# Two-block forward pass: the recurrent branch in 32x32 blocks with an explicit inverse, six heads a group, with 14 gate tiles and the memory's tiles between its matmuls

## The chip, the cores and the metric

The kernel runs on one core of a Trainium2 chip. The metric is the device time of one execution in microseconds (us). A core has TensorE (PE in the rows; PEld is its weight load), VectorE (DVE), ScalarE (ACT), GpSimd (POOL) and SyncE (SP), which issues most transfers. The engines run side by side and wait for one another by semaphores.

## What is computed

The reference is a model of two blocks over 512 tokens of width 1024. The change is in the second block, in one of its three branches and in what stands beside it:

```python
h = rms_norm(x, norm_mix_g)
(na_q, na_k, na_v, p_r, p_k, p_v, lat_w, lat_a, lat_g, mem_q,
 gate_na, gate_rw, gate_mem) = split_columns(h @ w_in)        # 1024 -> 5888 columns
y_na = neighborhood_attention(...)                            # 6 heads of 64
y_rw = rwkv7_bidirectional(...)                               # 6 heads of 64, two directions
y_mem = memory_attention(mem_q, rms_norm(mem), w_mem_kv)      # 256 memory tokens, 4 heads
merged = sigmoid(gate_na) * (y_na @ w_na) + sigmoid(gate_rw) * (y_rw @ w_rw) + sigmoid(gate_mem) * (y_mem @ w_mem)
x = x + merged @ w_out
x = x + expert_choice_ffn(rms_norm(x), ...)                   # 16 experts
```

The recurrence, for each head, each direction and each token in order:

```python
sa = einsum('vk,k->v', state, a_t)
state = state * w_t + outer(sa, b_t) + outer(v_t, k_t)        # 64 x 64
y_t = einsum('vk,k->v', state, r_t)
```

Then y of both directions is summed, normed by head, added to a bonus and multiplied by a gate.

## The kernel before

The program is a row of stages, each with a barrier at its end: the first block (projections, a state space branch, a gated recurrence, merge and feed-forward), then `front` (projections of the second block and the preparation of the recurrent branch), `attentions` (the two attention branches), `rwkv7` (the recurrent branch), `merge_and_router` and `expert_ffn`. Every large product is three fp32r matmuls (`three_passes`, L68 to L70): high by low, low by high, high by high.

`front` makes 46 tiles of 128 columns by 512 tokens and then 4 tiles of the memory's keys and values by 256 tokens. A tile is 8 steps of three matmuls. For each tile ACT makes the high half of the weights (L2351), DVE the low half (L2507), and DVE evicts the result (L2549). The preparation of the two directions for the recurrent branch runs beside tiles 6 to 18 and 19 to 31; its last piece is the bonus (L2642, L2644). Gate tiles are the last 24 of the 46.

`rwkv7` cuts the tokens into chunks of 32. Inside a chunk the recurrence is a triangular system. The work goes by units: 2 directions x 4 tiles of 128 tokens x 3 pairs of heads = 24 units. The four chunks of a tile lie as diagonal blocks in 128x128 matrices, masked to zero elsewhere (`masks`, L3054). A unit turns four operands (L2905), makes scores (L2911), turns the masked matrix (L2922), and solves the system in five levels (`level`, L2943 to L2945): each level squares the matrix and its transpose and adds A times z to z. To have the sums by chunk, POOL multiplies tokens by a membership mask (`split`, L2816). `finish` (L2964 to L2979) makes for each chunk the transfer matrix (`ht`), its addition (`nn`), the query part (`qt`) and the local output (`y_loc`). Then the scan: 15 steps x 2 directions, each a matmul of the state by the transfer matrix (L3019), one by the queries (L3027), and two DVE operations (L3119, L3122). At last the tail: mean and variance by head through matmuls with a block matrix of ones (L3034, L3037), a logarithm and an exponential on ACT (L2886, L2890), and three DVE operations for each of three tiles. In the tail DVE also splits the attention outputs for the merge, which came back from DRAM (L3134, L3136).

`attentions` runs 20 units (12 windowed, 8 of the memory). Its outputs are stored to DRAM (L1898).

The order on each engine is written out by hand in these functions; semaphores hold them together. The main loop of `rwkv7` on TensorE reads:

```python
for n in range(len(units)):
    level(n, 0)
    if n >= 1: finish(n - 1, 0)
    level(n, 1)
    if n >= 1: finish(n - 1, 1)
    level(n, 2)
    if n + 1 < len(units): front_a(n + 1)
    level(n, 3)
    if n + 1 < len(units): front_b(n + 1)
    level(n, 4)
```

Of the kernel before, what the change touches and what calls it, by code (L numbers as in the profile page):

```python
# [9 lines left out]
P = 128  # L10
ALU = mybir.AluOpType
# [1807 lines left out]
def attentions(nc, stage, na_dram, mem_q_dram, mem_kv_dram, bias_dram, ident_dram, na_out_dram, mem_out_dram):  # L1819
# [11 lines left out]
    with ExitStack() as ctx:  # L1831
# [38 lines left out]
        stored = sem("stored")  # L1870
# [10 lines left out]
        with nc.Block() as block:  # L1881

            @block.sync
            def _(sp):
# [10 lines left out]
                for o, (kind, c) in enumerate(outs):  # L1895
                    sp.wait_ge(y_ready, QT * (o + 1))
                    to = na_out_dram if kind == "na" else mem_out_dram
                    sp.dma_start(to[c * P:(c + 1) * P, :], y[kind][:, c]).then_inc(stored, 16)  # L1898
                sp.wait_ge(stored, 16 * len(outs))
# [77 lines left out]
            def _(dve):  # L1977
# [44 lines left out]
                for n in range(AHEAD):  # L2022
                    soften(n)
                    if n >= 1:
                        weigh(n - 1)
                for n in range(U):
# [4 lines left out]
                    finish(n)  # L2031

            @block.scalar
            def _(act):
# [26 lines left out]
                turned(0)  # L2061
                for n in range(U):
                    if n + 2 < U:
                        exponentials(n + 2)
                    if n + 1 < U:
                        turned(n + 1)

# [38 lines left out]
FRONT_MEM = 33  # L2106


def front(nc, stage, h_dram, mem_dram, gains_dram, mem_gain_dram, w_dram, par_dram, mu_l_dram, lora_dram, ar, bh, kh, v, bonus,
          ends, lat_g, x_dram, p_dram, kv_dram):  # L2110
# [5 lines left out]
    TM = N_MEM  # L2116
    tiles = FRONT_TILES + MEM_TILES
    with ExitStack() as ctx:
        sb, ps, sem = opener(nc, ctx, stage)
        x_high = sb("x_high", [P, KT, T], F32R)  # L2120
        x_low = sb("x_low", [P, KT, T], F32R)
# [4 lines left out]
        scale = sb("scale", [P, T])  # L2126
# [24 lines left out]
        mem = room[:, 0:KT * TM].rearrange("p (k t) -> p k t", k=KT)  # L2151
        mem_sq = room[:, KT * TM:KT * TM + KT * TM // 2].rearrange("p (k t) -> p k t", t=TM)
        mem_sums = sb("mem_sums", [P, 2, TM])
        mem_scale = sb("mem_scale", [P, TM])
        mem_gain = sb("mem_gain", [P, KT])
        with nc.sbuf_tensor(f"{stage}_raw", [P, 3, RW_X, T + 2], F32) as raw, nc.sbuf_tensor(f"{stage}_raw_l", [P, T + 2], F32) as raw_l:
            pass
# [1876 lines left out]
```

## Time and profile before

| what | us |
|---|---|
| median of 3 runs (lowest, highest) | 2938.48 (2933.32, 2939.51) |
| the profiled execution | 2938.72 |
| its span | 2936.3 |

By the rows' own times the second block begins near 1155 us of the span. `front` works until 1448, `attentions` has its first matmul at 1462.25 and its last eviction at 1518.99, `rwkv7` has its units from 1528 to 1803, its scan to 1828 and its tail to 1845, `merge_and_router` goes to about 1952, and the experts take the rest, 984 us, in which the transfer queues are 97% busy. Over the whole span TensorE is busy 91%, VectorE 43%, ScalarE 27%, GpSimd 4%.

How to read it: a matmul's row gives start and modelled length, but matmuls overlap; the distance from one start to the next is what it costs in a stream. A matmul on plain fp32 stands as two records, one on fp32r as one, and so does a transpose. `128*64 128x64` is a weight of 128 rows by 64 columns and a moving operand of 128 rows by 64 columns. Idle time of an engine that isn't the bound costs nothing.

### The profile page before, as it was taken

To read this page: it belongs to the slowest core of one execution; us is meant where nothing else is said; L and a number is where in the kernel's file an instruction comes from. 1 tells how busy PE (TensorE), PEld (TensorE's weight loads), DVE (VectorE), ACT (ScalarE), POOL (GpSimd) and SP (SyncE) were. 2 spreads that over 40 slices of the span, in tenths; PEclk is the share of its full clock that TensorE was granted. 3 is DMA by queue.
4 is the path that set the end of the run, shared out by engine and by line. 5 is a ranking of instruction groups with operands and counts; after the bars stand their busy time and mean duration, and the time that the engine had idled before them with its cause. 6 is when DMAs were issued, how large, how long until landed. Compare 5 with 4: busy or idle time off the path is not lost. (4 is left out here: it accounts for less than half of the span.)

```text
span 2936.3 us, 43512 instructions
## 1 busy us (share of the span) xinstructions
PE 2661.1 (91%) x18294; PEld 1902.3 (65%) x18294; DVE 1257.6 (43%) x2123; ACT 798.0 (27%) x1304; POOL 112.7 (4%) x90
## 2 busy tenths in 40 slices
PE   8997789799999998999789999879988898989887
PEld 8996677699999986778668887654333333333222
DVE  7764656544566633666353336750111111111112
ACT  3220454432343322543253333421000000000001
POOL 0000022000000000000002221000000000000000
PEclk9998899899999999999989999989999999999999
DMA  5447331455322233334510000548999999999996
GB/s 162 131 126 126 110 122 62 149 159 159 116 87 93 73 131 126 122 129 154 177 48 1 2 1 34 192 193 363 431 430 431 431 430 431 431 430 430 431 430 256
DMA packets 144432, 612.44 MB, mean 209 GB/s; under 512 B 37808, under 2 KB 57392, under 8 KB 119216
## 3 DMA queue, kind: packets, MB, share of 16 engines
q1 hardware_dynamic: 120576, 573.72, 50.9%
q10 hardware_dynamic: 23664, 35.95, 3.5%
q8 instruction: 146, 2.39, 0.3%
q14 instruction: 46, 0.38, 0.0%
HBM read 568.48 MB, written 38.78 MB: 207 GB/s over the span
## 5 line engine op out<-in xcount | busy, mean ns | idle before, releaser
L3552 PE MATMUL moe_bank<-moe_ring,xg 128*64 128x512 f32 x2048 | 493.7, 626 | 91.0 <-DMA moe_ring<-in_w_exp_up 90.2
L3552 PEld LDWEIGHTS moe_bank<-moe_ring,xg 128*64 128x64 f32 x2048 | 155.8, 142 | 371.7 <-issue 363.0
L3781 DVE TENSOR_TENSOR moe_sg<-moe_sg,moe_bank 64x512 f32<-64x512 f32 x64 | 44.2, 690 | 584.6 <-ACT moe_sg L3672 584.6
L3580 PE MATMUL moe_bank<-moe_ring,moe_act_t 128*64 128x512 f32 x1024 | 230.6, 592 | 0.5 <-ACT moe_act_t L3679 0.5
L68 PE MATMUL ffn_prod<-ffn_x_low,ffn_w_high 128*128 128x258 f32 x704 | 199.8, 284 | 5.8 <-PEq L144 5.8
L68 PE MATMUL in_bank<-x_low,in_w_high 128*128 128x264 f32 x640 | 186.9, 292 | 16.5 <-DVE in_w_low L983 9.3
L69 PE MATMUL ffn_prod<-ffn_x_high,ffn_w_low 128*128 128x258 f32 x704 | 199.7, 284 | 0.0
L70 PE MATMUL ffn_prod<-ffn_x_high,ffn_w_high 128*128 128x258 f32 x704 | 198.9, 283 | 0.0
L70 PE MATMUL in_bank<-x_high,in_w_high 128*128 128x264 f32 x640 | 184.0, 287 | 0.0
L69 PE MATMUL in_bank<-x_high,in_w_low 128*128 128x264 f32 x640 | 183.7, 287 | 0.0
L3580 PEld LDWEIGHTS moe_bank<-moe_ring,moe_act_t 128*64 128x64 f32 x1024 | 73.3, 137 | 146.4 <-issue 145.8
L3679 ACT COPY moe_act_t<-moe_bank 128x256 f32<-128x256 f32 x64 | 23.8, 372 | 515.9 <-PE moe_bank L3566 515.9
L68 PE MATMUL front_bank<-front_x_low,front_w_high 128*128 128x512 f32 x368 | 148.0, 402 | 12.3 <-DVE front_w_low L2507 12.2
L3789 DVE TENSOR_TENSOR acc<-acc,moe_bank 128x512 f32<-128x512 f32 x128 | 82.1, 683 | 174.3 <-PE moe_bank L3605 174.3
L69 PE MATMUL front_bank<-front_x_high,front_w_low 128*128 128x512 f32 x368 | 144.3, 392 | 0.0
L70 PE MATMUL front_bank<-front_x_high,front_w_high 128*128 128x512 f32 x368 | 144.1, 391 | 0.0
L68 PEld LDWEIGHTS ffn_prod<-ffn_x_low,ffn_w_high 128*128 128x128 f32 x704 | 133.6, 190 | 6.0 <-issue 6.0
L70 PEld LDWEIGHTS ffn_prod<-ffn_x_high,ffn_w_high 128*128 128x128 f32 x704 | 134.0, 190 | 0.0
L69 PEld LDWEIGHTS ffn_prod<-ffn_x_high,ffn_w_low 128*128 128x128 f32 x704 | 133.9, 190 | 0.0
L68 PEld LDWEIGHTS in_bank<-x_low,in_w_high 128*128 128x128 f32 x640 | 122.5, 191 | 17.6 <-issue 9.9
L69 PEld LDWEIGHTS in_bank<-x_high,in_w_low 128*128 128x128 f32 x640 | 123.1, 192 | 0.9 <-issue 0.8
L70 PEld LDWEIGHTS in_bank<-x_high,in_w_high 128*128 128x128 f32 x640 | 122.8, 192 | 0.0
(549 smaller groups left out, 5498.1 us busy)
## 6 DMA issues: line engine op xcount, KB each, us to landing
moe_ring<-in_w_exp_gate SPq DMA_DIRECT2D x64, 2048.0 KB, 27.6
moe_ring<-in_w_exp_up SPq DMA_DIRECT2D x64, 2048.0 KB, 21.3
moe_ring<-in_w_exp_down SPq DMA_DIRECT2D x64, 2048.0 KB, 25.8
front_w<-in_w_in SPq DMA_DIRECT2D x50, 512.0 KB, 3.6
ffn_w<-in_w_up SPq DMA_DIRECT2D x44, 512.0 KB, 4.5
in_w<-in_w_in SPq DMA_DIRECT2D x40, 512.0 KB, 4.2
ffn_w<-in_w_down SPq DMA_DIRECT2D x16, 704.0 KB, 4.0
p<-front_out ACTq DMA_DIRECT2D x35, 256.0 KB, 2.0
```

What stands on the lines that cost most here:

```text
L68: nc.tensor.matmul(to, w_high, x_low, start=start, stop=False)
L69: nc.tensor.matmul(to, w_low, x_high, start=False, stop=False)
L70: return nc.tensor.matmul(to, w_high, x_high, start=False, stop=stop)
L3552: last = nc.tensor.matmul(bank[64 * g:64 * g + 64, s], xe[:, (e // BATCH) % 2, k, at:at + CAPACITY], ring[:, slot_of(n, g), k * HALF:(k + ...
L3580: last = nc.tensor.matmul(bank[64 * h:64 * h + 64, 3 + e % 2], act_t[:, s, j], ring[:, slot, at:at + HALF], start=(c == 0 and j == 0), sto ...
L3679: nc.scalar.copy(act_t[:, s].rearrange("p j n -> p (j n)"), bank[:, 2, s * FT * CAPACITY:(s + 1) * FT * CAPACITY]).then_inc(act_t_ready, 1)
L3781: nc.vector.tensor_tensor(sg[0:CAPACITY, s], sg[0:CAPACITY, s], bank[64:64 + CAPACITY, s], ALU.mult).then_inc(act_ready, 1)
L3789: nc.vector.tensor_tensor(acc[:, FT * h + q], acc[:, FT * h + q], bank[:, part_bank(e, q) + h], ALU.add).then_inc(part_added, 1)
```

## The change

`front` makes only the first 10 gate tiles: 32 tiles in all, no memory tiles. Its rounded operands `x_high` and `x_low`, the scale and the identity are kept for the next stage.

`rwkv7` now comes before `attentions`. Its work goes by groups: 2 directions x 4 tiles of 128 tokens = 8 groups of all six heads. Tokens lie on partitions, 32 to a chunk, so each of the four chunks has its own 32 partitions, and every matrix of a chunk is a 32x32 block at those partitions; the other blocks don't exist, and no membership mask is needed. The system is solved through an explicit inverse: `ch` holds A transposed (AT), the product (PT) and A for each head; five rounds (`chain_round`, L3066, L3070) square A and multiply PT by (I + A^(2^l)). `solve` (L3079) applies the inverse to both right hand sides, `finish_ends` (L3095 to L3106) and `finish_rows` (L3118, L3123) make what `finish` made. Results go where the operands were: the transfer matrices into `ar`, the additions into `bh` and `kh`, the queries into `v`.

Between these pieces TensorE makes `side` work: 14 gate tiles and the 4 memory tiles, 18 x 8 = 144 steps of three matmuls, of which 9 in each group, 2 in each of 30 scan slots, and 3 x 4 in the tail. ACT and DVE split the weights and evict (`side`, `memory`).

`attentions` comes last before the merge. It splits its outputs and the recurrent branch's on chip into `x_high` and `x_low` (8 copies on ACT, 8 subtractions on DVE), loads and splits the first weights of the merge, and stores nothing.

The core of the diff (`...` marks what is left out):

```diff
+FRONT_GATES = 10
+FRONT_UPTO = FRONT_TILES - 3 * KT + FRONT_GATES
-    tiles = FRONT_TILES + MEM_TILES
+    tiles = FRONT_UPTO
...
+SIDE_GATES = 3 * KT - FRONT_GATES
+SIDE_FIRST = 4
+SIDE_TILES = SIDE_GATES + MEM_TILES
+RW_GROUPS = 2 * (SEQ // P)
+GROUP_STEPS = (2, 2, 2, 1, 2)
+SCAN_STEPS = 2
+TAIL_STEPS = 4
+SIDE_STEPS = GROUP_STEPS * RW_GROUPS + (SCAN_STEPS,) * (2 * (RSTEPS - 1)) + (TAIL_STEPS,) * 3
...
             @block.tensor
+                def side(slot):
+                    for q in range(SIDE_UPTO[slot], SIDE_UPTO[slot + 1]):
+                        n, k = divmod(q, KT)
+                        s = n % 2
+                        if k == 0:
+                            pe.wait_ge(w_ready, n + 1)
...
+                            done = three_passes(nc, bank[:, s], w_high[:, s, k], w_low[:, s, k], x_high[:, k], x_low[:, k],
+                                                k == 0, k == KT - 1)
...
+                def chain_round(g, l):
+                    now = ch[:, g % 2, l % 2]
...
+                    first = AT.start if l < LEVELS - 2 else PT.start
+                    upto = AT.stop if l == 0 else PT.stop
+                    for n in range(heads_all):
+                        at = 2 * RCHUNK * n
+                        for c in range(4):
+                            last = nc.tensor.matmul(bank[rows(c), CHAIN_BANK, at + first:at + upto], now[rows(c), n, A],
+                                                    now[rows(c), n, first:upto], start=True, stop=True)
+                        if l < LEVELS - 1:
+                            for c in range(4):
+                                last = nc.tensor.matmul(bank[rows(c), CHAIN_BANK + 1, n * RCHUNK:(n + 1) * RCHUNK], now[rows(c), n, AT],
+                                                        now[rows(c), n, A], start=True, stop=True)
+                    last.then_inc(round_made, 1)
...
+                for g in range(G):
+                    slot = len(GROUP_STEPS) * g
+                    chain_round(g, 0)
+                    if g >= 1:
+                        finish_ends(g - 1)
+                    side(slot)
+                    chain_round(g, 1)
+                    side(slot + 1)
+                    chain_round(g, 2)
+                    if g >= 1:
+                        finish_rows(g - 1)
+                    side(slot + 2)
+                    chain_round(g, 3)
+                    if g + 1 < G:
+                        turn(g + 1, 0)
+                        turn(g + 1, 1)
+                    side(slot + 3)
+                    chain_round(g, 4)
+                    if g + 1 < G:
+                        turn(g + 1, 2)
+                    side(slot + 4)
+                    if g + 1 < G:
+                        scores(g + 1)
+                    solve(g)
+                    if g + 1 < G:
+                        starts(g + 1)
...
             @block.vector
+                def inverse(g, l):
+                    dve.wait_ge(round_made, LEVELS * g + l + 1)
+                    made = bank[:, CHAIN_BANK, 0:2 * heads_all * RCHUNK].rearrange("p (n f) -> p n f", f=2 * RCHUNK)
+                    if l < LEVELS - 2:
+                        nc.vector.tensor_copy(ch[:, g % 2, (l + 1) % 2, :, AT], made[..., AT]).then_inc(inverse_ready, 1)
+                    if l == 0:
+                        return
...
+                    nc.vector.tensor_tensor(ch[:, g % 2, (l + 1) % 2, :, PT], ch[:, g % 2, l % 2, :, PT], made[..., PT],
+                                            ALU.add).then_inc(inverse_ready, 1)
```

On TensorE, in the middle of the second stage of the second block: one unit of before, from its last levels' neighbours to the next unit's first level (`rw_sm` is the masked matrix, `rw_power` its powers, `rw_z` the solution).

```order
L2945 MATMUL rw_bank<-rw_z,rw_power 128x128
L2905 MATMUL rw_bank<-rw_ident,rw_bh 128x128
L2905 MATMUL rw_bank<-rw_ident,rw_kh 128x128
L2905 MATMUL rw_bank<-rw_ident,rw_ar 128x128
L2905 MATMUL rw_bank<-rw_ident,rw_v 128x128
L2911 MATMUL rw_bank<-rw_ar,rw_bh 128x256 x2
L2911 MATMUL rw_bank<-rw_ar,rw_kh 128x256 x2
L2944 MATMUL rw_bank<-rw_power 128x128
L2945 MATMUL rw_bank<-rw_z,rw_power 128x128
L2944 MATMUL rw_bank<-rw_power 128x128
```

And of the change, the end of the second round of a group, the side work and the start of the third (`rw_ch` holds the blocks AT, PT and A of all heads).

```order
L3066 MATMUL rw_bank<-rw_ch 32x64 x4
L3070 MATMUL rw_bank<-rw_ch 32x32 x4
L68 MATMUL rw_bank<-rw_x_low,rw_w_high 128x512
L69 MATMUL rw_bank<-rw_x_high,rw_w_low 128x512
L70 MATMUL rw_bank<-rw_x_high,rw_w_high 128x512
L68 MATMUL rw_bank<-rw_x_low,rw_w_high 128x512
L69 MATMUL rw_bank<-rw_x_high,rw_w_low 128x512
L70 MATMUL rw_bank<-rw_x_high,rw_w_high 128x512
L3066 MATMUL rw_bank<-rw_ch 32x64 x4
L3070 MATMUL rw_bank<-rw_ch 32x32 x4
```

The whole-array fp32 products of a unit are gone from there; small blocks stand in their place, and the full-width fp32r products of the gate tiles, which stood in `front`, lie between two rounds.

On TensorE in the scan, before: the step and the query product of one direction follow those of the other at once.

```order
L3019 MATMUL rw_bank<-rw_states,rw_ht 64x64 x6
L3027 MATMUL rw_bank<-rw_qt,rw_states 64x32 x6
L3019 MATMUL rw_bank<-rw_states,rw_ht 64x64 x6
L3027 MATMUL rw_bank<-rw_qt,rw_states 64x32 x6
```

Of the change, one scan slot and the start of the next.

```order
L3171 MATMUL rw_bank<-rw_states,rw_ar 64x64 x6
L3178 MATMUL rw_bank<-rw_v,rw_states 64x32 x6
L68 MATMUL rw_bank<-rw_x_low,rw_w_high 128x512
L69 MATMUL rw_bank<-rw_x_high,rw_w_low 128x512
L70 MATMUL rw_bank<-rw_x_high,rw_w_high 128x512
L68 MATMUL rw_bank<-rw_x_low,rw_w_high 128x512
L69 MATMUL rw_bank<-rw_x_high,rw_w_low 128x512
L70 MATMUL rw_bank<-rw_x_high,rw_w_high 128x512
L3171 MATMUL rw_bank<-rw_states,rw_ar 64x64 x6
```

The matmuls of a slot are the same; two steps of a gate tile now stand behind them.

On VectorE in `attentions`, of the change, the end of one windowed unit and the next (`att_s` the scores, `merge_x_low` the merge's operand).

```order
L2021 COPY att_y<-att_bank 128x8x16
L2042 TENSOR_TENSOR merge_x_low<-att_y,merge_x_high 128x512
L1997 SCALAR_TENSOR_TENSOR att_s<-att_bank,att_bias 128x512
L2002 TENSOR_REDUCE att_low<-att_s 128x2
L2006 RECIPROCAL att_inverse<-att_total 128x2
L2013 TENSOR_SCALAR att_weights<-att_ident,att_inverse 128x128 x2
L2021 COPY att_y<-att_bank 128x8x16
```

The subtraction at L2042 is new there; the six other operations are those of before.

## Rows read from the trace of the kernel before

**Rows 1.** Busy time by stretch: stretch, length, PE, PEld, DVE, ACT, POOL, clock, DMA share, GB/s.
```profile
1462.00:1520.00 58.00, 54.15 (x428) 38.92 (x428) 42.90 (x120) 37.17 (x113) 0.00 (x0) 0.94 0.20 73
1528.00:1803.00 275.00, 264.83 (x2723) 227.76 (x2723) 102.89 (x262) 84.22 (x191) 60.02 (x48) 0.98 0.01 1
1845.20:1851.20 6.00, 5.94 (x14) 4.72 (x15) 3.13 (x5) 4.67 (x6) 0.00 (x0) 0.50 0.84 286
```

**Rows 2.** Timeline, `front`'s end: start, length, engine, line, operation, idle before and its releaser.
```profile
1359.51 0.68 DVE L2549 TENSOR_TENSOR front_out<-front_bank,front_scale 128x512 f32<-128x512 f32 x1
...
1430.38 0.69 DVE L2549 TENSOR_TENSOR front_out<-front_bank,front_scale 128x512 f32<-128x512 f32 x1 [3.07 <-PE front_bank L70]
...
1435.82 0.69 DVE L2549 TENSOR_TENSOR front_out<-front_bank,front_scale 128x512 f32<-128x512 f32 x1 [3.07 <-PE front_bank L70]
...
1447.65 0.42 DVE L2552 TENSOR_TENSOR front_out<-front_bank,front_mem_scale 128x256 f32<-128x256 f32 x1 [2.85 <-PE front_bank L70]
...
1450.23 0.44 ACTq L2036 DMA_DIRECT2D att_q<-p  x1
```

**Rows 3.** Timeline of TensorE, small matmuls in the first block and in the scan.
```profile
200.50 0.28 PE L70 MATMUL in_bank<-x_high,in_w_high 128*128 128x264 f32 x1
200.71 2.03 PE L743 MATMUL in_bank<-s_ca,in_bb 64*32 64x128 f32 x128
202.68 0.39 PE L68 MATMUL in_bank<-x_low,in_w_high 128*128 128x264 f32 x1
202.91 0.28 PE L69 MATMUL in_bank<-x_high,in_w_low 128*128 128x264 f32 x1
...
1824.83 0.56 PE L3019 MATMUL rw_bank<-rw_states,rw_ht 64*64 64x64 f32 x12
...
1826.63 0.84 PE L3027 MATMUL rw_bank<-rw_qt,rw_states 64*64 64x32 f32 x24
```

**Rows 4.** Timeline of TensorE, the same place in two units of `rwkv7`.
```profile
1651.62 0.27 PE L2905 MATMUL rw_bank<-rw_ident,rw_bh 128*128 128x128 f32 x1
...
1662.76 0.27 PE L2905 MATMUL rw_bank<-rw_ident,rw_bh 128*128 128x128 f32 x1
1662.87 0.27 PE L2905 MATMUL rw_bank<-rw_ident,rw_kh 128*128 128x128 f32 x1
```

**Rows 5.** Timeline in `rwkv7`: its first transfer, the masks' first use, the scan.
```profile
1521.71 0.33 SPq L2796 DMA_DIRECT2D rw_ident<-in_ident  x1
...
1526.63 1.29 DVE L3054 TENSOR_TENSOR rw_sm<-rw_bank,rw_masks 128x512 f32<-128x512 f32 x2 [4.16 <-PE rw_bank L2911]
...
1825.11 0.36 DVE L3122 TENSOR_TENSOR rw_states<-rw_states,rw_ends 128x192 f32<-128x192 f32 x1
```

**Rows 6.** Timeline, the end of the scan and the tail.
```profile
1827.65 0.54 PE L3027 MATMUL rw_bank<-rw_qt,rw_states 64*64 64x32 f32 x12 [0.17 <-DVE rw_states L3122]
...
1829.07 2.81 PE L3034 MATMUL rw_bank<-rw_y,rw_blocks 128*128 128x512 f32 x6 [0.88 <-DVE rw_y L3127]
...
1832.53 3.09 DVE L3134 TENSOR_TENSOR merge_x_low<-rw_x_raw,merge_x_high 128x512 fp32r<-128x512 f32 x5
...
1836.45 1.28 ACT L2890 ACT_TABLE_LOAD   x1
...
1844.24 0.69 DVE L3147 TENSOR_TENSOR rw_bonus<-rw_y,rw_split 128x512 f32<-128x512 f32 x1
```

**Rows 7.** Timeline of VectorE in `attentions`: one windowed unit.
```profile
1491.94 0.69 DVE L1993 SCALAR_TENSOR_TENSOR att_s<-att_bank,att_bias 128x512 f32<-128x512 f32 x1
...
1492.67 0.69 DVE L1998 TENSOR_REDUCE att_low<-att_s 128x2 f32<-128x512 f32 x1
...
1493.46 0.48 DVE L2009 TENSOR_SCALAR att_weights<-att_ident,att_inverse 128x128 f32<-128x128 f32 x2
...
1493.86 0.28 DVE L2017 COPY att_y<-att_bank 128x128 f32<-128x128 f32 x1
...
1494.25 0.69 DVE L1993 SCALAR_TENSOR_TENSOR att_s<-att_bank,att_bias 128x512 f32<-128x512 f32 x1
```

More of the change, by code:

```diff
@@ L2689, in _ @@
                         prepare(d, i)
-                    memory(n - FRONT_MEM)
                     if n >= 4:
@@ L2874, in _ @@
                         bonus_ready, 1)
[L2875 to L2879 removed]
+                slot = scan_slot(1, 0)
+                while slot < len(SIDE_STEPS):
+                    side(slot)
+                    slot += 1
+                for last in range(len(SIDE_STEPS) - 2, len(SIDE_STEPS)):
+                    for n in ended(last):
+                        store(n)
                 for x in range(RW_X):
@@ new lines, in starts @@
+                def starts(g):
+                    pe.wait_ge(masked, 4 * (g + 1))
+                    pe.wait_ge(tok_ready, RW_X * (g + 1))
+                    for n in range(heads_all):
+                        for c in range(4):
+                            last = nc.tensor.matmul(bank[rows(c), FIRST_BANK, n * HEAD_DIM:(n + 1) * HEAD_DIM],
+                                                    rec[rows(c), g % 2, n, KA], rec[rows(c), g % 2, n, V_TOK], start=True, stop=True)
+                    last.then_inc(z0_made, 1)
@@ new lines, in solve @@
+                def solve(g):
+                    pe.wait_ge(inverse_ready, INVERSES[-1] * (g + 1))
+                    pe.wait_ge(z0_ready, g + 1)
+                    for n in range(heads_all):
+                        for c in range(4):
+                            last = nc.tensor.matmul(bank[rows(c), CHAIN_BANK + n // 4, n % 4 * P:(n % 4 + 1) * P],
+                                                    ch[rows(c), g % 2, LEVELS % 2, n, PT], rec[rows(c), g % 2, n, 3 * FIELD:RECORD],
+                                                    start=True, stop=True)
+                    last.then_inc(z_made, 1)
@@ L2963, in finish @@
                         for e in range(2):
-                            nc.tensor.matmul(bank[heads(e), 5, 0:256], ww[e], split[:, s, 0, :, heads(e)], start=True,
-                                             stop=True)
+                            for c in range(4):
+                                n = 2 * x + e
+                                nc.tensor.matmul(bank[heads(e), END_BANK + c, at:at + HEAD_DIM], of[rows(c), n, B_TOK],
+                                                 of[rows(c), n, ZZ], start=True, stop=False)
@@ L2966, in finish @@
                         for e in range(2):
-                            nc.tensor.matmul(bank[heads(e), 5, 256:384], ww[e], sm[:, s, e, 1], start=True, stop=True)
-                    for c in (0, 1) if part == 0 else (2, 3):
+                            for c in range(4):
+                                n = 2 * x + e
+                                last = nc.tensor.matmul(bank[heads(e), END_BANK + c, at:at + HEAD_DIM], of[rows(c), n, K_TOK],
+                                                        of[rows(c), n, V_TOK], start=False, stop=True)
@@ L3138, in _ @@
+                side(len(SIDE_STEPS) - 1)
+                for n in ended(len(SIDE_STEPS) - 1):
+                    finish_side(n)
                 dve.wait_ge(bonus_ready, RW_X)
```

970 lines of the change are left out of this document (538 added, 432 removed).

## The prediction, made before the changed kernel ran

> **What bounds the kernel now.** I first read the busy time by stretch [rows 1]. In the units of `rwkv7` TensorE is busy 264.8 of 275 us, with VectorE at 102.9 and ScalarE at 84.2: what counts there is how long its matmuls are in a row. The projections of `front` are a plain stream: the reader is to see two evictions 5.44 us apart [rows 2], which is 24 matmuls at 0.227. In `attentions` VectorE's operations follow each other with no gap and come back after 2.31 us [rows 7], so VectorE sets the pace there. The experts after the merge start only when it ends and aren't touched: what the second block saves before the merge is saved in full.
>
> So I lay the new second block out in time, from the last point that stays to the start of the merge, which is at 1845.2 before [rows 1], and compare. All times are of the profiled execution; it took 2938.72 us for a span of 2936.3, and the median of the runs is 2938.48, so its sum carries over.
>
> **The end of `front`.** The tiles up to 31 stay as they are. Tile 31 is evicted at 1359.51 for 0.68, behind the bonus of the second direction [rows 2]. Now that is the end of the stage. From the last eviction's end (1447.65 + 0.42) to the first transfer of the next stage passed 2.16 us [rows 2]; the same again gives 1362.3. The 14 + 4 tiles that were cut had filled 88 us.
>
> **The start of `rwkv7`.** Before, the first masking came 4.9 us after the first transfer [rows 5]. The masks are smaller now but queue behind a 512 KB weight tile, so I take the same; then four masking operations (0.4 us each) and one set of first products on a slow clock: 6.6 us, so the first round starts at 1368.9. Turns and scores of the first group lie under the wait.
>
> **A group.** From the code, in matmuls: 12 turns; 72 for scores, 24 for starts, 48 + 48 + 48 + 48 + 24 for rounds, 72 and 48 for the two finishes, so 432 small ones; 24 in `solve` with 128 columns; 27 of side work. No row shows a 32x32 block with 32 or 64 moving columns. The nearest: 128 records of 64x32 blocks with 128 columns take 1.97 us from the first start to the next work's, about 13.9 ns a record, and a matmul is two records, so 27.8 ns [rows 3]. In the scan 64x64 blocks with 64 columns have 31 ns a record ((0.56 - 0.22) / 11) and with 32 columns 27 ns ((0.84 - 0.22) / 23) [rows 3]. A record of the whole array with 128 columns costs 110 ns [rows 4], so 64 columns would be 55 alone: two blocks side by side ran at half of that, and eight blocks of the first case at an eighth of 110. A 64-column block on the diagonal has three neighbours: a quarter of 55 is 13.8, the same 27.8 ns a matmul. For 32 columns the array would allow half, 13.9 ns a matmul, if the records can be issued so fast, which no row shows. Bounds: 13.9 and 54 ns. I take 27.8 for all 432, since it is the rate of the row with the smallest blocks.
>
> - 432 x 27.8 ns = 12.0 us; `solve` 24 x 55 ns = 1.3; turns 12 x 0.11 = 1.3 [rows 4].
> - side work 27 x 0.227 = 6.1.
> - going from whole-array matmuls to blocks and back: the first block starts 0.21 after the last whole one, where 0.12 is usual, and on the way back 0.2 and then 0.11 are lost [rows 3]: 0.4 for the two. Five such trips and four changes between block shapes of 0.1: 2.4. Ends: nothing, and twice that.
> - waits: between two rounds lie a copy and a sum on VectorE (192 columns: 0.36 [rows 5]) and one copy on ScalarE. With the semaphores 1.0 us, under 1.4 us of side work; in slot 3 the turns cover it. At the end of a group masking (1.9 us after the scores) outlasts `solve` by 0.6.
>
> Sum 23.7; eight groups 189.6. Off go 4.0 (the first group's turns, scores and starts, done already) and 9.9, since four of the tiles are memory tiles, which took (1447.65 - 1435.82) / 4 = 2.96 and not 5.44 [rows 2]. That is 175.7. Where a new side tile starts in the first two slots, VectorE has its reading of ends (about 2 us) and the weights' split (twice a 0.62 piece [rows 6]) ahead of the inverse, and the round is 0.9 late: five groups, 4.5. The groups end at 1549.1. Before, 24 units at 11.14 [rows 4] were 267. VectorE has some 9.5 us in a group of 23.7 and ScalarE less; POOL's masks are gone, and nobody had waited for them.
>
> The last group's finish has no cover: right sides, ends, reading, rows, about 5.7. 1554.8.
>
> **The scan.** A slot was 0.34 + 0.30 of matmuls [rows 3]. Now 6 side matmuls (1.36) and a trip (0.4) stand behind each, 2.4 in all, and 30 slots are 72.0. VectorE's 0.7 a slot, which had stood in the chain (1.41 a step for both directions), is under the other direction's slot. With a weights' split in one slot of four it has 1.2 on average. 1626.8.
>
> **The tail.** Before, from the last query product's start to the last operation's end, 17.3 us [rows 6]. In it go the five subtractions, which nothing had waited for (ScalarE's table load and exponentials ended later). On come 12 side steps of 0.68, of which the first 4 and two gate products (0.87 each, as six records took 2.6 us [rows 6]) partly lie over VectorE's sums. I count the chain anew: gate products and four steps 4.4, means 2.6, eight steps 5.4, variance 0.9, logarithms 1.8, table 1.3, exponential 0.6, three by three operations 6.4, semaphores 1.3: 24.7. 1651.5, and 0.3 to the next stage.
>
> **`attentions`.** It took 71.5 us from its first transfer to the next stage's (1450.2 to 1521.7) [rows 2, 5]. VectorE gets 8 subtractions of 0.62 [rows 6] and one of 1.2. VectorE has no gap [rows 7], so 7 x 0.62 + 1.2 = 5.5 are on the path; ScalarE, busy 37 of 58 us [rows 1], has room for its copies. At the end a copy and a subtraction (1.3) replace the landing of the last store (1519.3 to 1521.7: 2.4). Net +4.4: 75.9, so the merge starts at 1727.7. Ends: 0 and 6.2 more.
>
> **The merge.** It began on the half clock: 0.50 over 1845.2 to 1851.2 [rows 1], where 14 matmuls took 0.43 each. Now TensorE has worked until some 1.5 us before, and I take the full clock: -2.8. Ends: -2.8 and 0.
>
> Sum: 1845.2 - 1727.7 + 2.8 = 120.3 saved. 2938.7 - 120.3 = **2818 us**.
>
> One rule of the Trainium skill speaks to the largest term. "TensorE: Matmul & The Clock Gate", section "Wait — 56ns, not 53.3ns?", says that start to start never falls below about 25 ns, however small the matmul. By the rule a small matmul of two records would be 50 ns and the groups 77 us longer; an estimate by that page, 2895. Rows 3 contradict it with 13.9 ns over 128 records; its 27 ns with 64-column weights are in line with it.
>
> **The rivals.**
>
> *Records at the scan's price.* If the 27 ns of the 32-column products are not the loading of 64-column weights but the least that a small matmul costs, 432 x 8 x 26.6 ns = +92: 2910. For it: it is the only row with 32 columns. Against it: half that price in the other row, with a larger moving operand. The rule of the Trainium skill's TensorE page above would come out near this case.
>
> *Cheaper blocks.* With 13.9 ns where there are 32 columns or eight blocks at once (288 of 432): -32, 2786. Nothing speaks against it but that nothing shows such a rate.
>
> *One PSUM bank at a time.* If blocks of different rows couldn't write one bank together, rounds, starts and `solve` run alone: in a group 168 x 55 + 72 x 110 + 24 x 220 ns = 22.4 us where I have 8.0. +115: 2933, within 0.2%. In the scan both heads' blocks write one bank and go at half the price of one alone [rows 3], which speaks against it. This is a gotcha of the Trainium skill, "TensorEngine Tiling (Array Packing)", "Gotcha 1: PSUM Pressure": row tiles can't access one bank at the same time. Rows 3 disagree for two tiles on different partitions; no row has four.
>
> *Slower: no packing on the diagonal.* If the 32-row blocks don't overlap at all, a group's matmuls are 240 x 55 + 168 x 110 + 24 x 165 + 24 x 220 ns = 41 us where I have 13.3: +222, 3040. Place: every round and finish. It decides from 62.6 ns a small matmul on (27.8 + 120.3 us / 3456). Against it: the eightfold packing in rows 3.
>
> **How the numbers follow.** The forecast has 0.71, with a range of its own from 2790 to 2860 (trips between none and double are -31 and +31, the waits up to 2 us more in a group, +16). Cheaper blocks 0.09, the scan's price 0.13, one bank 0.03, no packing 0.04. The range of 8 in 10 takes the forecast's whole range, the cheaper case and some of the way to the dearer: 2780 to 2885. A measurement of this kernel can tell about 0.2%, 5.9 us, from no change. Faster: 0.71 + 0.09 + 0.13 and a little of one bank, 0.94; the same 0.02; slower 0.04.
>
> **What would show it.** In the changed profile: the last eviction of `front` near 1360; two first turns of groups about 23.7 us apart (two thirds of the old time for three units, 33.4), in it 48 matmuls of a round in about 1.3 us, with a record every 14 ns (7, 27 or 55 for the rivals); slots of the scan 2.4 apart; a windowed unit of `attentions` still 2.31 except where a subtraction of 0.62 stands in it; the merge's first matmuls at 0.23, not 0.43. If TensorE waits more than 2 us in a group for VectorE or ScalarE, the step on the waits is wrong, and if the first block or the experts move by over 2 us, so is the frame.

## The result, and the profile of the changed kernel

The changed kernel takes 2874.4 us (median of 4 runs, 2867.6 to 2876.8), the kernel before 2938.8 (4 runs beside it, 2933.3 to 2939.5). The ratio is 0.978, with a 95% interval of 0.977 to 0.980: 64 us saved, where 120 had been forecast. The profiled executions show the same: spans of 2873.3 and 2936.3, 63.0 apart. The time is within the range, 57 us over the forecast, and 48.6 us of the miss lie in one stretch, the groups.

Busy time of the changed kernel by stretch (columns as in [rows 1]): the groups, the last finish, the scan, the tail, `attentions`, and the merge's first 6 us.

```profile
1365.00:1598.00 233.00, 179.96 (x7314) 151.46 (x7316) 72.43 (x169) 56.57 (x112) 0.00 (x0) 0.83 0.14 44
1598.00:1609.80 11.80, 8.31 (x321) 5.74 (x309) 3.09 (x8) 4.60 (x8) 0.00 (x0) 0.90 0.01 3
1609.80:1683.20 73.40, 73.40 (x877) 55.69 (x877) 34.42 (x74) 7.33 (x7) 0.00 (x0) 0.97 0.24 70
1683.20:1710.70 27.50, 15.71 (x53) 9.52 (x51) 10.44 (x16) 7.75 (x11) 0.00 (x0) 0.86 0.08 28
1710.70:1784.30 73.60, 54.62 (x428) 39.09 (x429) 50.34 (x141) 43.39 (x123) 0.00 (x0) 0.87 0.28 105
1784.30:1790.30 6.00, 5.98 (x19) 4.83 (x20) 1.28 (x2) 3.82 (x3) 0.00 (x0) 0.72 0.80 295
```

In the groups TensorE works 180 of 233 us. It had been busy 96% of the units before [rows 1]; now it is 77%, while VectorE has 72 us and ScalarE 57 in 233, so neither is the bound. The granted clock fell with it, from 0.98 to 0.83.

What TensorE waits for in this stretch, from the view of waits (total us, times, longest); three of the rows with "issue", and all three that name VectorE or ScalarE:

```profile
PE rw_bank L3070 <- issue: 8.1, 5, 3.2
PE rw_bank L3066 <- issue: 7.7, 10, 1.4
PE rw_bank L3101 <- issue: 6.5, 3, 2.2
...
PE rw_bank L3048 <- DVE rw_ch L3251: 3.2, 2, 2.1
...
PE rw_bank L3066 <- ACT rw_ch L2907: 1.0, 1, 1.0
PE rw_bank L3066 <- ACT rw_rec L2928: 0.8, 2, 0.4
```

VectorE and ScalarE hold it for 5.0 us in eight groups. "Issue" means that it waited for nothing that the profile shows. Stops of at least 0.5 us of this kind are 33, with 45.6 us.

Where they fall is the clue. Timeline of TensorE in the changed kernel, parts of one group (start, length, line, count, and in brackets the idle time before):

```profile
1472.92 0.29 PE L3123 MATMUL rw_bank<-rw_rec 32*64 32x32 f32 x6
1474.54 0.25 PE L3123 MATMUL rw_bank<-rw_rec 32*64 32x32 f32 x3 [1.32 <-issue]
...
1477.07 0.19 PE L3066 MATMUL rw_bank<-rw_ch 32*32 32x32 f32 x1
1478.22 0.23 PE L3066 MATMUL rw_bank<-rw_ch 32*32 32x32 f32 x3 [0.97 <-issue]
...
1478.47 0.33 PE L3020 MATMUL rw_bank<-rw_ident,rw_bh 128*128 128x128 f32 x1
...
1479.85 0.62 PE L3066 MATMUL rw_bank<-rw_ch 32*32 32x32 f32 x48
...
1483.55 0.22 PE L3039 MATMUL rw_bank<-rw_bh,rw_ar 64*32 64x32 f32 x2 [1.21 <-issue]
...
1487.41 0.74 PE L3079 MATMUL rw_bank<-rw_rec,rw_ch 32*32 32x128 f32 x18 [1.74 <-issue]
...
1491.23 0.27 PE L3070 MATMUL rw_bank<-rw_ch 32*32 32x32 f32 x3 [0.81 <-issue]
...
1495.10 0.38 PE L3106 MATMUL rw_bank<-rw_rec 32*64 32x64 f32 x3 [1.25 <-issue]
```

The stops fall in the middle of loops, in six different lines, not at a change of shape nor at a wait in the code. From restart to restart it is 3.86, 3.82 and 3.87 us at the end of this list. The same three stretches by engine:

```profile
1483.54:1487.40 3.86, 2.12 (x127) 1.81 (x128) 1.71 (x5) 0.00 (x0) 0.00 (x0) 1.00 0.02 4
1487.40:1491.22 3.82, 3.02 (x127) 2.92 (x127) 0.56 (x1) 0.86 (x2) 0.00 (x0) 0.58 0.02 4
1491.22:1495.09 3.87, 2.61 (x127) 2.36 (x127) 0.36 (x1) 0.32 (x1) 0.00 (x0) 0.50 0.02 4
```

Each holds 127 or 128 matmul records and as many weight loads: 256 instructions. And the queues on the page of the changed kernel, with TensorE's counts:

```profile
PE 2550.9 (89%) x22950; PEld 1793.0 (62%) x22950; DVE 1199.4 (42%) x2001; ACT 752.3 (26%) x1203; POOL 49.1 (2%) x41
...
q8 instruction: 182, 2.98, 0.4%
```

On the page of the kernel before:

```profile
PE 2661.1 (91%) x18294; PEld 1902.3 (65%) x18294; DVE 1257.6 (43%) x2123; ACT 798.0 (27%) x1304; POOL 112.7 (4%) x90
...
q8 instruction: 146, 2.39, 0.3%
```

A packet of the instruction queue is 2.98 MB / 182 = 16 KB. The change adds 2 x 4656 = 9312 instructions on TensorE, and 36 packets: 9216 is 36 x 256. So a block of 256 instructions is one packet, and a stop looks like the wait for the next one. The trace holds the time of each packet of this queue, and the stops can be laid beside them. For the three stretches above (us):

| TensorE restarts | next packet starts | that packet ends | TensorE restarts |
|---|---|---|---|
| 1483.55 | 1484.66 | 1486.13 | 1487.41 |
| 1487.41 | 1488.64 | 1489.82 | 1491.23 |
| 1491.23 | 1492.78 | 1493.73 | 1495.10 |

It is so at every stop: in all 33, TensorE starts again 1.21 to 1.57 us after a packet of this queue has ended, and the next packet starts no sooner than 1.04 us after that. So a stop is the wait for a packet, and the next packet sets out only when TensorE has gone into a new block: one packet is under way at a time, one block ahead. The 3.8 us are the sum of three legs, with medians of 1.24 us to the packet's start, 1.15 for the packet and 1.41 from its end to the restart (22 stretches of one block). What fills the first and the last leg no row shows.

The stretches above also show what a stop isn't: in the first TensorE had the full clock, in the third the half, with the same period, and data moved at 4 GB/s.

**Theory A** from here: TensorE gets 256 instructions in no less than about 3.8 us (the 22 one-block periods between two stops in the groups have a median of 3.85, from 3.40 to 5.33). A group has 468 matmuls of two records (1872 instructions) and 27 side matmuls (54), 1926 in all, 7.5 blocks; at 3.8 us that is 28.6. The six distances between the first turns of full groups are 28.1 to 31.5, with a mean of 29.6. **Rival B**: the stops belong to a place or to the change between whole-array matmuls and blocks, and the price is by record. **Rival C**: each 256th instruction costs a stop of about 1.4 us whatever lies between.

### The profile page after: what moved, and what is told of

Read it like the earlier page. It is cut to its first block and busy times, and to the rows that moved or that the text cites. A ratio compares the mean times of both kernels' runs of the same rounds, so it can differ in the third digit from the quotient of the medians.

```text
span 2873.3 us, 52189 instructions
## 1 busy us (share of the span) xinstructions
PE 2550.9 (89%) x22950; PEld 1793.0 (62%) x22950; DVE 1199.4 (42%) x2001; ACT 752.3 (26%) x1203; POOL 49.1 (2%) x41
## 3 DMA queue, kind: packets, MB, share of 16 engines
q8 instruction: 182, 2.98, 0.4%
## 5 line engine op out<-in xcount | busy, mean ns | idle before, releaser
L68 PE MATMUL front_bank<-rw_x_low,front_w_high 128*128 128x512 f32 x256 | 105.4, 412 | 12.8 <-DVE front_w_low L2497 12.8
L70 PE MATMUL front_bank<-rw_x_high,front_w_high 128*128 128x512 f32 x256 | 101.7, 397 | 0.0
L69 PE MATMUL front_bank<-rw_x_high,front_w_low 128*128 128x512 f32 x256 | 101.7, 397 | 0.0
## 6 DMA issues: line engine op xcount, KB each, us to landing
moe_ring<-in_w_exp_gate SPq DMA_DIRECT2D x64, 2048.0 KB, 27.6
```

Of the source, the lines that this page charges most:

```text
L68: nc.tensor.matmul(to, w_high, x_low, start=start, stop=False)
L69: nc.tensor.matmul(to, w_low, x_high, start=False, stop=False)
L70: return nc.tensor.matmul(to, w_high, x_high, start=False, stop=stop)
```

## The experiments

Below, "groups" is the time from the first turn to the gate product behind the last finish: 242.8 us in the changed kernel (1365.0 to 1607.8).

**72 small matmuls more in a group (x1_more).**

```diff
                         for c in range(4):
+                            for _ in range(3):
+                                nc.tensor.matmul(bank[rows(c), FIRST_BANK, n * HEAD_DIM:n * HEAD_DIM + 1],
+                                                 rec[rows(c), g % 2, n, KA], rec[rows(c), g % 2, n, V_TOK][:, 0:1], start=True, stop=True)
                             last = nc.tensor.matmul(bank[rows(c), FIRST_BANK, n * HEAD_DIM:(n + 1) * HEAD_DIM],
```

> The changed kernel with 72 more small matmuls in a group (three of one column ahead of each of the 24 first products). Theory A, instruction supply: in the groups TensorE gets 256 instructions (128 matmul records and their 128 weight loads) in no less than about 3.85 us. 72 matmuls are 288 instructions, 1.125 x 3.85 = 4.3 us a group, 35 us in all: 2909. Theory B, the stops belong to a place or to a change between whole-array matmuls and blocks, and a record costs only what the dense runs show (7.5 ns): 144 x 7.5 ns = 1.1 us a group, 9 us in all: 2883.

Measured: 2907.3 us, ratio to before 0.990 (0.989 to 0.992); groups 274.2, 31.4 more. Theory A had 35 and B 9, but the run doesn't decide between them, since the trace shows another cause for the same number. The added matmuls stand one behind another on the same 32x32 block, where nothing overlaps. The first products of a group, with the additions, are 192 records in 4.1 to 6.0 us without stops, 22 to 31 ns a record and not 7.5; the 48 of the changed kernel take 0.7 to 1.4. Over eight groups that is 33 us more of TensorE's own time, and the stops didn't grow (37 with 43.5 us, for 33 with 45.6). That the number fell near Theory A is luck. What the run does show is the count: 191 packets of the instruction queue for 182, 9 more, and 8 x 288 / 256 = 9.

**Power products of all six heads in one matmul (x2_wide)**, and **the products with the inverse too (x2b_wide2)**. Both use the first head's weights for all heads, so the values are others.

```diff
-                        if l < LEVELS - 1:
-                            for c in range(4):
-                                last = nc.tensor.matmul(bank[rows(c), CHAIN_BANK + 1, n * RCHUNK:(n + 1) * RCHUNK], now[rows(c), n, AT],
-                                                        now[rows(c), n, A], start=True, stop=True)
+                    if l < LEVELS - 1:
+                        for c in range(4):
+                            last = nc.tensor.matmul(bank[rows(c), CHAIN_BANK + 1, 0:heads_all * RCHUNK].rearrange(
+                                "p (n f) -> p n f", f=RCHUNK), now[rows(c), 0, AT], now[rows(c), :, A], start=True, stop=True)
```

> The changed kernel with the power products of a round for all six heads in one matmul of 192 columns per chunk, instead of six of 32: the same columns, 80 matmuls (320 instructions) fewer in a group. The weights are those of the first head for all, so the values are another computation. Theory A: 1.25 x 3.85 = 4.8 us a group less, 38 us in all, 2836, or a few us over it where the other work of a group becomes the limit. Theory B: 160 records of 7.5 ns less, 1.2 us a group, 2865; if the columns are what counts, 2874.

> As the run with wide power products, and the products with the inverse too (weights of the first head for all): 180 matmuls, 720 instructions fewer in a group, same columns. Theory A: some 1200 instructions are 18 us at 3.85 us for 256, less than the other work (some 21 us without the stops), so nearly all stops go: 8 x 8 us = 64 less, 2810. Theory B: 360 records of 7.5 ns, 2.7 us a group, 2852; 2874 if columns count.

Measured: 2844.3 us, ratio 0.969 (0.967 to 0.970), and 2814.3 us, ratio 0.959 (0.957 to 0.960). The stretch of the groups in the two, then the second one's queue:

```profile
1365.20:1577.40 212.20, 169.75 (x6330) 135.02 (x6330) 74.78 (x176) 60.58 (x120) 0.00 (x0) 0.90 0.16 48
```

```profile
1364.50:1547.00 182.50, 154.11 (x4731) 112.68 (x4731) 74.65 (x176) 60.66 (x120) 0.00 (x0) 0.97 0.17 55
```

```profile
q8 instruction: 160, 2.62, 0.4%
```

With the same columns and the same order of the stages the groups fall by 30.6 and 60.3 us. B would give 10 and 22. Packets go by 10 (172) and by 22 (160), as 8 x 320 / 256 = 10 and 8 x 720 / 256 = 22.5 say. Places and changes of shape are as before, and the stops fall from 33 with 45.6 us to 22 with 29.7 and 11 with 14.3: this pair decides against B. The stops are about half of what was gained, 16 and 31 us. The rest is TensorE's own busy time, 16 and 32 us less than the 186.3 of the changed kernel, more than B's 10 and 22 for the records alone, at a clock that came back to 0.90 and 0.97. The low clock was a consequence of the stops and not their cause: the period was 3.86 us at 1.00 of the clock and 3.87 at 0.50, above.

**More side work in the groups, less in the scan (x3_side15).**

```diff
-GROUP_STEPS = (2, 2, 2, 1, 2)
+GROUP_STEPS = (3, 3, 3, 3, 3)
-SIDE_STEPS = GROUP_STEPS * RW_GROUPS + (SCAN_STEPS,) * (2 * (RSTEPS - 1)) + (TAIL_STEPS,) * 3
+SIDE_STEPS = GROUP_STEPS * RW_GROUPS + ((4,) + (0,) * 9) * 3 + (TAIL_STEPS,) * 3
```

The memory's tiles start two tiles later here, and in the next run two earlier, so that what they need is there.

> The changed kernel with 15 side steps in each group (not 9) and 12 instead of 60 in the scan. Theory A: the groups are held by instructions, of which six side steps are only 36, 0.5 us, so they grow by 4 to 10 us in all, while the scan falls to the chain of its states (1.41 us for both directions, 15 x 1.41 = 21, and three times 3 us of side work): from 73 to 30. 2874 - 43 + 7 = 2838. Theory B: the groups grow by 6 x 0.7 x 8 = 34 us: 2865. If VectorE becomes late in the groups, above 2865.

Measured: 2851.8 us, ratio 0.972 (0.970 to 0.974), between the two theories. From its first to its last state product the scan fell from 67.3 to 30.9 us; the groups grew by 15.0, of the 34 us of work put into them. Of the 19 us that don't show, the stops took in 10 (25 stops with 35.9 us are left), and 8 went with the clock: it was 0.88 and not 0.84, and TensorE's busy time grew by only 26. So the stops take in less than I had said.

**Less side work in the groups (x4_side4).**

```diff
-GROUP_STEPS = (2, 2, 2, 1, 2)
+GROUP_STEPS = (1, 1, 1, 0, 1)
-SIDE_STEPS = GROUP_STEPS * RW_GROUPS + (SCAN_STEPS,) * (2 * (RSTEPS - 1)) + (TAIL_STEPS,) * 3
+SIDE_STEPS = GROUP_STEPS * RW_GROUPS + (3, 3, 4) * 10 + (TAIL_STEPS,) * 3
```

> The changed kernel with 4 side steps in each group (not 9) and 100 instead of 60 in the scan. 17 us of side work stay in the groups of the changed kernel's 39, so 22 us move to the scan. Theory A, a least period for 256 instructions: the stops take up what the side work leaves, the groups fall only by its instructions, 240 in all, 3.5 us: 2874 + 22 - 3.5 = 2893. Theory C, a stop of some 1.4 us at each 256th instruction whatever lies between: the groups fall by the whole 22 us: 2874.

Measured: 2885.0 us, ratio 0.983 (0.981 to 0.984). The groups fell by 10.9 us of 22, again between. C is wrong in its plain form: the stops grew from 45.6 to 49.8 us (36 of them) with the side work gone. A is wrong too in the size that it gave them. TensorE's busy time fell by only 16 of the 22 us, at a clock of 0.79 for 0.84. A holds with a condition, which the packets' times above show: the supply runs only one block ahead, so side work hides in a stop of its own block and not in one three blocks later. The one-block periods have a median of 3.69 here (22, from 3.30 up), a little shorter than with more work in them.

**The side work in nine places (x5_spread15, x7_spread16, x10_spread9).** The core of the edit, on TensorE (the other engines' calls follow it):

```diff
                     chain_round(g, 0)
+                    side(slot)
                     if g >= 1:
                         finish_ends(g - 1)
-                    side(slot)
+                    side(slot + 1)
...
                         scores(g + 1)
+                    side(slot + 6)
                     solve(g)
+                    side(slot + 7)
                     if g + 1 < G:
                         starts(g + 1)
+                    side(slot + 8)
```

> 15 side steps a group as in the run before (2852), but in nine places and not five: also between the scores, the inverse's use, the first products, the first round and the first finish, where some 960 instructions had stood in a row with no side work between them. Theory A with the period kept for each block of 256 instructions by itself: that run's groups took 15 us more than the changed kernel's since side work fell where no stop was; spread, most of this goes: 2840. If the instructions are only short on average over a group: 2852, unchanged. If VectorE or the waits for it set the groups by now: 2852 or above.

> The spread form with 16 side steps a group and 4 in the scan. 8 steps leave the scan (5.4 us) with two trips (0.8 us). Theory A: the groups still have stops to hide 0.7 us each in: 6 us under the spread form with 15, 2834. If no stops are left there: the same as that form.

> The changed kernel's 9 side steps a group and 2 a slot in the scan, but the 9 in nine places, one each. In the changed kernel a block of 256 instructions takes 28.1 / 7.5 = 3.75 us on average over a group, as between two stops. Theory A (the supply sets the mean over a group already): nothing to gain from the places, 2870 to 2875. Theory D (the gain of the spread form with 15 steps was one of the places by themselves): 10 us less, 2864.

Measured: 2841.9 us, ratio 0.968 (0.966 to 0.969), with 15 steps; 2832.8, 0.965 (0.963 to 0.967), with 16; 2872.9, 0.979 (0.977 to 0.981), with 9. The first beats the same 15 steps in five places by 10 us, as the block-by-block reading says, and the last is not faster than the changed kernel, so the places by themselves, Theory D, are worth nothing. (The 28.1 us in this run's expectation is the shortest of the six full groups; their mean of 29.6 is 3.9 us a block.) In the trace of the form with 16 the groups are these, with TensorE busy 85% and the clock at 0.94:

```profile
1364.90:1615.20 250.30, 213.81 (x7778) 172.16 (x7779) 87.40 (x190) 66.82 (x127) 0.00 (x0) 0.94 0.20 61
```

**24 MB more traffic in the groups (x6_load), and 4 MB less (x11_quiet).**

```diff
+                    if 2 <= n < 10:
+                        for m in range(12 * (n - 2), 12 * (n - 1)):
+                            if m >= 2:
+                                sp.wait_ge(junk_loaded[m % 2], 16 * (m // 2))
+                            sp.dma_start(junk[:, m % 2], w_dram[m % 32 * P:(m % 32 + 1) * P, 0:512]).then_inc(junk_loaded[m % 2], 16)
```

```diff
+                    upto = D_MODEL if n < 2 or n > 9 else 16
-                    sp.dma_start(w[:, n % 2].rearrange("p k m -> p (k m)"), w_dram[w_row(n) * P:(w_row(n) + 1) * P, :]).then_inc(
-                        w_loaded[n % 2], 16)
+                    sp.dma_start(w[:, n % 2].rearrange("p k m -> p (k m)")[:, 0:upto],
+                                 w_dram[w_row(n) * P:(w_row(n) + 1) * P, 0:upto]).then_inc(w_loaded[n % 2], 16)
```

> The changed kernel with 12 more transfers of 256 KB, two at a time, for each of 8 side tiles, into a buffer that nobody reads: some 24 MB more in the groups. The first stops, at 268 GB/s of traffic, were 3.2 us and later ones 1.0 to 2.2 us. Theory A1, the instructions come over the same DMA engines as data and wait behind it: the period grows towards 5.5 us where the load runs, 3 to 6 us a group, 2900 to 2920. Theory A2, the supply is limited at its own end: within 5 us of 2874.

> The changed kernel with only 16 of 1024 columns of the side weights loaded for the eight tiles from the third on: 4 MB less traffic in the groups (the values of these tiles are not the reference's). The other side of the run with 24 MB more. In the changed kernel three stops in a row came 3.8 us apart at 5 GB/s, and the same at 72. Theory A2, 3.8 us is the supply's own time and light traffic doesn't add to it: 2870 to 2875. Theory A1, every transfer beside it adds in proportion (the added 24 MB cost 13 us): 2 us less, 2872, which the times can't tell from A2; if the weights' bursts are what makes the stops, 2860 or less.

Measured: 2887.7 us, ratio 0.983 (0.981 to 0.985), with more, and 2870.9, 0.978 (0.977 to 0.980), with less. Three periods of the loaded kernel:

```profile
1428.90:1433.60 4.70, 2.70 (x127) 2.36 (x127) 0.56 (x1) 0.86 (x2) 0.00 (x0) 0.63 0.50 158
1433.60:1438.30 4.70, 2.62 (x127) 2.33 (x127) 0.36 (x1) 0.32 (x1) 0.00 (x0) 0.50 0.38 116
1478.90:1483.70 4.80, 2.72 (x126) 2.30 (x127) 1.23 (x1) 1.52 (x2) 0.00 (x0) 1.00 0.38 124
```

The same 256 instructions take 4.7 to 4.8 us at 116 to 158 GB/s (median of all one-block periods 4.57, against 3.85), with TensorE busy for 2.6 to 2.7 of them. So instructions do come through something that data transfers share, and the packets show where: in the one-block periods the next packet started up to 3.3 us after the restart (median 1.52, against 1.24), single packets took up to 2.5 us (1.5 at most without the load), and the last leg stayed (median 1.32). By the medians the run is 13 us slower, a third to a half of what A1 had; its profiled execution was its fastest, 2879.6, and the groups in it grew by 8.5. With less traffic the period stays at 3.83 (19 of them, 4.12 at most), as the rows at 4 GB/s say: 3.8 us is the supply's own. The groups are 237.3 in that trace, 5.5 less, which the times can't tell from nothing. One reading in the last expectation is wrong: no stop came 3.8 us apart at 72 GB/s. That was the mean of ten us, and the stretch in them, 1483.54 to 1487.40, had 4. In the changed kernel too, where a weight tile's 0.5 MB passed ahead of the packet, the packet started 3.1 and 2.6 us after the restart, and the periods were 5.33 and 4.95.

**The last places (x8_finish, x9_groups17).** The spread form with 16 steps and 4 more between the last group's two finishes; then 17 steps and 4 instead of 12 in the tail.

```diff
                 finish_ends(G - 1)
+                side(len(GROUP_STEPS) * G)
                 finish_rows(G - 1)
```

```diff
-GROUP_STEPS = (2, 2, 2, 2, 1, 2, 2, 2, 1)
+GROUP_STEPS = (2, 2, 2, 2, 2, 2, 2, 2, 1)
-SIDE_STEPS = GROUP_STEPS * RW_GROUPS + (4,) + (0,) * (2 * (RSTEPS - 1)) + (TAIL_STEPS,) * 3
+SIDE_STEPS = GROUP_STEPS * RW_GROUPS + (4,) + (0,) * (2 * (RSTEPS - 1)) + (0, TAIL_STEPS, 0)
```

> The spread form with 16 side steps a group (2833), and the 4 steps that the scan had left put between the last group's two finishes, where TensorE waits 1.8 us for VectorE. The scan gets 2.7 us and a trip of 0.4 shorter, the finish 2.7 + 0.4 - 1.8 longer: 2831. If the stops for instructions fall there too, 2829.

> As the run before, with 17 side steps a group and 4 instead of 12 in the tail. 8 steps are 5.4 us. If the stops in the groups still take a step in (there were 24 stops and 30 us with 16): 2826. If the groups are at the length of their own work by now, what the tail loses the groups gain: 2831.

Measured: 2837.2 us, ratio 0.967 (0.965 to 0.969), and 2830.2, 0.964 (0.962 to 0.966). The first is no better than the form with 16 steps, its interval overlaps; its groups with the four steps took 261.1 for 250.3, where I had counted 1.3 more, and the rest of that is unexplained. Traces of the groups scatter by some us: the form with 9 steps in nine places had 248.8 in its profiled execution for 242.8, with equal medians. The second is the fastest of the runs with the reference's values, 44 us under the changed kernel and 107 under before, though not told apart from the form with 16.

## Why the prediction came out as it did

By its own steps, in the profiled execution; the misses add up to the 57.3 us between 120.3 and 63.0.

| step | forecast | measured | miss |
|---|---|---|---|
| `front` to the first transfer | 1362.3 | 1365.0 | +2.7 |
| to the first round | 6.6 | 8.3 | +1.7 |
| groups and last finish | 185.9 | 234.5 | +48.6 |
| scan, with the gate product ahead | 72.0 | 75.4 | +3.4 |
| tail, to the next transfer | 25.0 | 27.6 | +2.6 |
| `attentions` | 75.9 | 73.5 | -2.4 |
| clock of the merge and rest | -2.8 | -2.1 | +0.7 |

**The frame held.** The last eviction of `front` and the start of the second block, beside [rows 2, 5]:

```profile
1361.84 0.69 DVE L2538 TENSOR_TENSOR front_out<-front_bank,rw_scale 128x512 f32<-128x512 f32 x1 [1.44 <-PE front_bank L70]
```

```profile
1364.96 0.33 SPq L2846 DMA_DIRECT2D rw_w<-in_w_in  x1
...
1372.01 1.50 PE L3048 MATMUL rw_bank<-rw_rec 32*32 32x64 f32 x48 [2.07 <-DVE rw_ch L3251]
```

Two us of it were there in the eviction six tiles earlier (1331.52 for 1329.68), which I haven't followed up.

**Small matmuls: the mechanism was right, and the price near.** Blocks on the diagonal do overlap. With 64 columns the 48 records of the first products took 0.66 us where they were densest (1426.86 to 1427.52), 14 ns each, the rate that I took. With 32 columns they overlap more: in the timeline above 48 records of a round start within 0.62 - 0.19 us, 9 ns apart, between my 14 and the cheap rival's 7. A mixed round of 96 records took 1.18 (1471.22 to 1472.40), for some 1.3 in the forecast. Without their stops the six full groups have a mean of 29.6 - 5.9 = 23.7 us, the forecast's own figure. That it is so exact is luck: the records of 32 columns were cheaper than I had them, and the clock was 0.83 and not the 0.98 that I had left it at. "One bank at a time", "the scan's price" and "no packing" are all ruled out by these rates.

**The step that failed is "Sum 23.7; eight groups 189.6": a group was priced as a sum of matmul times, trips and waits, and the supply of its instructions was put at nothing.** The stops in it were 45.6 of the stretch's 48.6 us of miss. "432 x 27.8 ns = 12.0 us" is the line that hid it. It carried the rate of one row [rows 3] over to 432 matmuls. That row has 128 records, and with their weight loads 256 instructions, as many as one block, followed by whole-array work. It could not show what a second and third block cost. A group has 7.5 blocks, whose supply alone takes 7.5 x 3.8 = 28.6 us, and that is a bound beside the sum: the longer of the two counts, block by block. That the time still fell into the range is luck, since no rival named this cause. The nearest, the scan's price, had 27 ns a record for the record itself; a dense stretch comes out near it (3.8 us / 128 = 30 ns) for the other reason.

The Trainium skill's rule in "TensorE: Matmul & The Clock Gate", section "Wait — 56ns, not 53.3ns?", of about 25 ns start to start is not what the rows show for blocks side by side, which take 9 and 14 ns. Small matmuls behind one another on one block (the run with 72 more) took 22 to 31 ns a record, near that rule.

**Waits in a group: right.** 5.0 us in eight groups for VectorE and ScalarE, of which 2.1 stand ahead of the first round; the inverse's chain was covered by side work.

**Scan: right.** The first products of two slots in a row start 2.40 us apart, the forecast's own figure, and TensorE has no idle time in the stretch:

```profile
1631.03 0.56 PE L3171 MATMUL rw_bank<-rw_states,rw_ar 64*64 64x64 f32 x12
...
1633.43 0.56 PE L3171 MATMUL rw_bank<-rw_states,rw_ar 64*64 64x64 f32 x12
```

I left out the first gate product, 2.0 us on the path.

**Tail and `attentions`.** The tail was 2.6 longer. In `attentions` the splits cost what was said. The starts of two units without one are 2.11 apart (and 2.37 with the next), with a subtraction between them 2.71 [rows 7]:

```profile
1741.62 0.69 DVE L1997 SCALAR_TENSOR_TENSOR att_s<-att_bank,att_bias 128x512 f32<-128x512 f32 x1
...
1743.53 0.28 DVE L2021 COPY att_y<-att_bank 128x128 f32<-128x128 f32 x1
1743.73 0.68 DVE L1997 SCALAR_TENSOR_TENSOR att_s<-att_bank,att_bias 128x512 f32<-128x512 f32 x1
...
1748.81 0.69 DVE L1997 SCALAR_TENSOR_TENSOR att_s<-att_bank,att_bias 128x512 f32<-128x512 f32 x1
...
1750.92 0.68 DVE L2033 TENSOR_TENSOR merge_x_low<-rw_bonus,merge_x_high 128x512 fp32r<-128x512 f32 x1
1751.52 0.68 DVE L1997 SCALAR_TENSOR_TENSOR att_s<-att_bank,att_bias 128x512 f32<-128x512 f32 x1
```

It came to 73.5 for 75.9. Most of it is in the unit that I had expected "still 2.31": without a subtraction it takes 2.11. From the start of its last copy to the next scores it is 0.20 us here and was 0.39 before [rows 7], so those rows were not VectorE at its closest, as I had read them. What closed the 0.2 us stays open, and so does the rest of the 2.4.

**The merge's clock: half right.** It started at the full clock, fell back for seven matmuls and rose again:

```profile
1784.62 0.39 PE L69 MATMUL merge_bank<-merge_x_high,merge_w_low 128*128 128x512 f32 x1
...
1785.59 0.63 PE L69 MATMUL merge_bank<-merge_x_high,merge_w_low 128*128 128x512 f32 x1
...
1788.96 0.39 PE L69 MATMUL merge_bank<-merge_x_high,merge_w_low 128*128 128x512 f32 x1
```

Shown: a dense stretch of small matmuls is limited by the supply of its instructions in blocks of 256, one packet each, one block ahead (the packets' times, their counts in five kernels, the two wide forms). Neither the clock nor the columns set it, and data traffic lengthens it. The 3.8 us are the three legs of one packet's round. Not settled: what fills the 1.2 us before a packet and the 1.4 us behind it.

## What to carry to other kernels

Count instructions, not only matmul times: an fp32 matmul is four here (two records, two weight loads), and a dense stretch went at about 3.8 us for each 256 (never under 3.3), however small they were. Where packing in blocks makes a stretch denser than that, long matmuls from elsewhere are cheap in it if they are spread so that each block of 256 gets its share (15 steps in nine places made the groups 9.3 us longer for 34 us of work, the same in five places 15); fewer, wider instructions gained 30 and 60 us here with the columns unchanged. And a rate read from one short row holds for its length only: ask how many instructions it had.

## What the runs showed that I had not expected

- Stops of 0.5 to 3.2 us after 256 instructions, with periods from 3.3 us up and a median of 3.85; 4.6 with 12 extra transfers of 256 KB a tile running. In the changed kernel each of the 33 stops ended 1.2 to 1.6 us after a packet of the instruction queue had.
- Records of 32x32 blocks with 32 columns start 9 ns apart inside a block of instructions, four tiles on the diagonal writing one PSUM bank. Behind one another on one tile they took 22 to 31 ns.
- The stops lower the granted clock of the stretch (0.83, and 0.79 with 72 more matmuls in a group; 0.97 with 180 fewer), so side matmuls among them take longer too.
